# Summing the squares of the last RMS norm on TensorE, block by block, instead of on VectorE

## The chip, the cores and the metric

The kernel runs on one core of a Trainium2 chip. The metric is the device time of one execution in microseconds. Times of several runs are given by their median. A core has TensorE (matmuls, shown as PE, with its weight loads as PEld), VectorE (DVE), ScalarE (ACT), GpSimd (POOL) and SyncE (SP), each with its own queue in program order; they wait for each other by semaphores.

## The reference, cut to what matters

The program is two transformer blocks on 512 tokens of 1024 features. The second ends with a mixture of 16384 experts (PEER), whose output is added to the residual `x`, and the kernel ends with an RMS norm:

```
def rmsnorm_2(x, g):
    xf = x.astype(jnp.float32)
    y = xf * lax.rsqrt(jnp.mean(xf * xf, axis=-1, keepdims=True) + EPS)
    return (y * g.astype(jnp.float32)).astype(x.dtype)
...
        x = x + peer_ffn(h2, peer_w_query[l], peer_sub_keys[l], peer_u[l], peer_v[l])
    return rmsnorm_2(x, final_g)
```

All that changes is how the sum over the 1024 features of `xf * xf` is formed, once per token.

## The kernel before, in words

The residual is kept transposed in SBUF: `xT` has 128 partitions (features) x KD = 8 blocks x T = 512 tokens. So the squares of a token lie on 128 partitions in 8 blocks, and their sum goes over both.

The last stage adds the experts' output. It goes over 64 pairs of expert tiles (N_PAIRS). For each pair j, `mix` on TensorE makes the 8 blocks of the output with 6 matmuls each (L1786 to L1788, 128 x 128 stationary, 416 moving columns), into banks 0 to 3 in turn, and counts `y_done`. VectorE adds each block to `xT` and counts `y_added` (L1698, and L1772 for the last pair). ScalarE meanwhile prepares the next weights.

Behind the last pair comes the final norm. ScalarE squares block k as soon as its residual addition is done (`square_tile`, L765) into one of three buffers: block 0 into `sq[:, 0]`, the others in turn into `sq[:, 1]` and `res`; from the third buffer's reuse on it waits for VectorE (`sq_added`). VectorE adds block k - 1 of squares to `sq[:, 0]` behind the residual addition of block k (`add_square`, L1238), seven additions in all. When the seventh is done (`squares`), TensorE sums over the partitions: `square_sums` (L1883) has one matmul for each 128 tokens, with the squares as the stationary operand and one column of ones as the moving one, and leaves four columns of bank 4. ScalarE takes the root (L699, with a table load), VectorE the reciprocal (L1174), TensorE spreads it over all partitions (`spread_roots`, L1875, four matmuls with 128 moving columns into bank 5), VectorE makes the eight final products (L1779), and ScalarE's queue stores each block when it is done (L1114).

Every engine runs its queue in order. On TensorE the final norm's instructions stand behind the matmuls of pair 63. The four buffers `rows[0..3]` (128 x 1024 each) take gathered expert rows in an earlier part of the stage; ScalarE waits for `acc_added` before it comes to the final norm.

Of the kernel before, what the change touches and what calls it, by code (L numbers as in the profile page):

```python
# [26 lines left out]
ACT = mybir.ActivationFunctionType  # L27
AX_X = mybir.AxisListType.X

P = 128  # L30
D = 1024
KD = D // P
T = 512
TT = T // P
# [162 lines left out]
def program(nc, x, stream, gains, consts, rel, gqa, keys, ohc, rows_u, rows_v, out):  # L197
    ctx = ExitStack()
    with ctx:
# [3 lines left out]
        def fixed(name, shape, dt=F32):  # L203
            size = int(np.prod(shape[1:])) * (2 if dt in (BF16, F16) else 4)
            if size % ROW == 0:
                at[0] = -(-at[0] // ROW) * ROW
            t = nc.alloc_sbuf_tensor_at(name, shape, dt, offset=at[0])
            at[0] += -(-size // 32) * 32
            return t

        def sem(name):
            return ctx.enter_context(nc.semaphore(name))


        xT = fixed("xT", [P, KD, T])
# [9 lines left out]
        rr = fixed("rr", [P, TT])  # L225
# [123 lines left out]
        rows = [fixed(f"rows{r}", [P, D]) for r in range(ROWS_AHEAD - 1)]  # L349
# [36 lines left out]
                    2: sq[:, 0, :], 3: sq[:, 1, :], 4: rt[:, 0, :], 5: pr1[:, 1, 0, :]}  # L386
        y_scaled = pr1[:, 0, 0, :]
        normed_of = lambda k: (res[:, :], rt[:, 0, :], sq[:, 1, :])[k % 3]
        sq_tile = lambda k: sq[:, 0, :] if k == 0 else sq[:, 1, :] if k % 2 else res[:, :]
        spilled = nc.dram_tensor("spilled", (N_SPILLED, P, DT), F32, kind="Internal").ap()  # L390
        gates = nc.dram_tensor("gates", (N_SPILL, P, NKEY, SPILL), F32, kind="Internal").ap()

        banks = ctx.enter_context(nc.psum_tensor("bank", [P, 8, T], F32))
        B = [banks[:, i, :] for i in range(8)]
# [13 lines left out]
        roots = sem("roots")  # L408
        recips = sem("recips")
# [77 lines left out]
        acc_turned = sem("acc_turned")  # L487
        acc_added = sem("acc_added")
        a_moved = sem("a_moved")
        gate_done = sem("gate_done")  # L490
        high_w = sem("high_w")

        ident = cs[:, CC["ident"]:CC["ident"] + P]
        ones = cs[:, CC["ones"]:CC["ones"] + P]
# [17 lines left out]
        def gain(name, k=0):  # L512
            return gn[:, GC[name] + k:GC[name] + k + 1]
# [162 lines left out]
        def _(act):  # L676
# [19 lines left out]
            def root_of(width, scale, n_sums):  # L696

                act.wait_ge(sums, n_sums)
                act.activation(rr[:, :width], B[4][:, :width], ACT.Sqrt, bias=gain("eps"), scale=scale).then_inc(roots, 1)  # L699
# [61 lines left out]
            def square_tile(nth, k, src=xT):  # L761

                if k >= 3:
                    act.wait_ge(sq_added, nth * (KD - 2) + k - 2)
                act.activation(sq_tile(k), src[:, k, :], ACT.Square).then_inc(squared, 1)  # L765
# [10 lines left out]
            n_sums = KD  # L776
# [87 lines left out]
            for m in range(AHEAD, N_IN2):  # L864
# [11 lines left out]
                o = 2 * g + r - 2 if m < 4 * KD else m - 2 * KD  # L876
# [230 lines left out]
            for k in range(KD):  # L1107

                act.wait_ge(y_added, (N_PAIRS - 1) * KD + k + 1)
                square_tile(2, k)  # L1110
            root_of(TT, 1.0 / D, n_sums + KD)
            for k in range(KD):
                act.wait_ge(final_done, k + 1)
                act.dma_start(out[:, k, :], xT[:, k, :]).then_inc(out_done, 16)  # L1114
# [4 lines left out]
        def _(dve):  # L1119
# [52 lines left out]
            def over_root(width, nth_root):  # L1172
                dve.wait_ge(roots, nth_root)
                dve.reciprocal(rr[:, :width], rr[:, :width]).then_inc(recips, 1)  # L1174
# [58 lines left out]
            def add_square(nth, k):  # L1233

                dve.wait_ge(squared, nth * KD + k + 1)
                if k >= 2:
                    dve.wait_ge(sq_added, nth * (KD - 2) + k - 1)
                ins = dve.tensor_tensor(sq_tile(0), sq_tile(0), sq_tile(k), ALU.add)  # L1238
                if k < KD - 1:
                    ins.then_inc(sq_added, 1)  # L1240
                else:
                    ins.then_inc(squares, KD)

            n_sums, n_root, n_spread = 0, 0, 0
# [267 lines left out]
            for k in range(KD):  # L1512
                t = c2[:, k, :]
# [256 lines left out]
            for k in range(KD):  # L1770
                dve.wait_ge(y_done, (N_PAIRS - 1) * KD + k + 1)
                dve.tensor_tensor(xT[:, k, :DT], xT[:, k, :DT], B[k % 4][:, :DT], ALU.add).then_inc(y_added, 1)  # L1772
                if k >= 2:
                    add_square(2, k - 1)
            add_square(2, KD - 1)
            over_root(TT, n_root + 1)
            dve.wait_ge(spread, n_spread + 1)
            for k in range(KD):
# [4 lines left out]
        def _(pe):  # L1783
# [87 lines left out]
            def spread_roots(bank=5):  # L1871

                for t in range(TT):
                    tok = slice(t * P, (t + 1) * P)
                    m = pe.matmul(B[bank][:, tok], rr[:, t:t + 1].broadcast_to([P, P]), ident, start=True, stop=True)  # L1875
                m.then_inc(spread, 1)

            def square_sums(n):


                pe.wait_ge(squares, n + KD)
                for t in range(TT):
                    m = pe.matmul(B[4][:, t:t + 1], sq[:, 0, t * P:(t + 1) * P], ones[:, 0:1], start=True, stop=True)  # L1883
                m.then_inc(sums, KD)

            def full_norm(n, nth):

                square_sums(n)
                pe.wait_ge(recips, nth)
                spread_roots()  # L1890
# [82 lines left out]
            n_sq, n_rt = 0, 0  # L1973
# [298 lines left out]
            for n in range(NB):  # L2272
                build(n)
                while at_step < tile_steps(n):
                    u, k = at_step // KD, at_step % KD
# [17 lines left out]
            def mix(j, wpar, n_lo, r):  # L2293

                pe.wait_ge(lo_done, n_lo)
                pe.wait_ge(w_done, j * 2 + 2)
                for k in range(KD):
                    if not isinstance(j, int) or j * KD + k - 3 > 0:
                        pe.wait_ge(y_added, j * KD + (k - 3))
                    c = slice(k * P, (k + 1) * P)  # L2300
                    for e in (0, 1):
                        m = mm3(B[k % 4][:, :DT], hi[:, r + e, c], lo[:, r + e, c], WH[:, wpar, e, :DT], WL[:, wpar, e, :DT],
                                e == 0, e == 1)
                    m.then_inc(y_done, 1)
# [54 lines left out]
            with pe.Fori(N_BOTH // 2, N_PAIRS // 2) as i:  # L2359
                for q in (0, 1):  # L2360
                    mix(i * 2 + q, q, i * 4 + (S_LAST - 2 * N_BOTH + 2 * q + 2), 2 * q)
            full_norm(n_sq, n_rt + 1)

        return None

# [120 lines left out]
```

## Time and profile before

| what | value |
|---|---|
| median of 3 runs | 2484.57 us (2475.71 to 2488.78) |
| profiled execution, its own time | 2480.68 us |
| its span | 2478.8 us |
| TensorE matmul busy | 2406.5 us (97%) |
| VectorE busy | 1686.6 us (68%) |
| ScalarE busy | 929.7 us (38%) |
| last wide matmul to the end of the span | 13.7 us |

The span runs from the first to the last record of the core; the own time includes what lies around it. Busy time is the union of an engine's instructions, and the durations of overlapping matmuls are more than their spacing. The trace shows two records (a load and a matmul, twice) for each 4-byte matmul of the final norm, so 4 matmuls appear as x8.

### The profile page before, as it was taken

What the parts mean: (1) busy time and instruction counts of PE and PEld (TensorE: products, weight loads), DVE (VectorE), ACT (ScalarE), POOL (GpSimd) and SP (SyncE); (2) the same over time, 40 slices, a digit from 0 to 9 for tenths busy, and PEclk for the clock granted to TensorE, in tenths of its full rate; (3) what the DMA queues carried; (4) which work ended last, traced back from release to release, by engine and by line L of the source; (5) the groups of instructions that cost most, each with busy time, mean ns of one, the idle gap of its engine ahead of it and who ended that gap; (6) DMA issues with size and microseconds to landing.
All of it is one profiled execution on the core that took longest, in us unless ns stands there. A gap on an engine that the chain in (4) does not pass through costs nothing.

```text
span 2478.8 us, 37450 instructions
## 1 busy us (share of the span) xinstructions
PE 2406.5 (97%) x13120; PEld 2162.0 (87%) x13120; DVE 1686.6 (68%) x3411; ACT 929.7 (38%) x1473; POOL 1333.1 (54%) x1185
## 2 busy tenths in 40 slices
PE   7999999999999999999998998999999999999998
PEld 6785788888888886788997887999999999999998
DVE  6476733332499977779999975666766766666666
ACT  3146222222322346414354553333333433433443
POOL 5520565656555562464410014777777777777553
PEclk9999999999999999999999998999999999999999
DMA  4210233223233222122225676877887887887552
GB/s 170 94 52 27 77 102 100 94 102 102 86 109 100 95 85 80 50 97 85 96 92 188 250 267 190 297 250 277 271 272 270 274 282 264 269 282 263 172 168 96
DMA packets 210870, 402.72 MB, mean 162 GB/s; under 512 B 118336, under 2 KB 123840, under 8 KB 207424
## 3 DMA queue, kind: packets, MB, share of 16 engines
q1 hardware_dynamic: 64224, 233.36, 28.1%
q0 software_dynamic: 27648, 100.68, 11.0%
q10 hardware_dynamic: 118880, 67.18, 9.1%
q8 instruction: 66, 1.08, 0.2%
q14 instruction: 52, 0.43, 0.1%
HBM read 369.25 MB, written 31.92 MB: 162 GB/s over the span
## 4 chain that ended last, share of the span: by engine, by line
PE 74%; DVE 17%; issue 3%; POOL 3%; ACT 1%; DMA 1%; DVEq 0%; POOLq 0%; SPq 0%; ACTq 0%
PE bank L1786 23%; PE bank L1787 23%; PE bank L1788 23%; POOL lo L600 3%; DVE ohg L1667 2%; DVE lo L1606 1%; DVE oh L1663 1%; DVE oh L1664 1%; PE bank L1944 1%; PE bank L1955 1%; PE bank L1931 1%; DVE idx L1565 1%; DVE inH L1133 1%; DVE idx L1557 1%; DVE scb L1558 1%
## 5 line engine op out<-in xcount | busy, mean ns | idle before, releaser
L600 POOL TENSOR_TENSOR lo<-raw,hi 128x256 fp32r<-128x256 f32 (+1 forms) x950 | 1135.2, 1224 | 1006.8 <-ACT hi L686 562.5
L1786 PE MATMUL bank<-inH,hi 128*128 128x512 f32 (+1 forms) x2112 | 790.2, 374 | 19.2 <-DVE inL L1134 14.0
L1788 PE MATMUL bank<-inH,lo 128*128 128x512 f32 (+1 forms) x2112 | 781.5, 370 | 0.0
L1787 PE MATMUL bank<-inL,hi 128*128 128x512 f32 (+1 forms) x2112 | 781.2, 370 | 0.0
L1786 PEld LDWEIGHTS bank<-inH,hi 128*128 128x128 f32 x2112 | 396.5, 188 | 69.5 <-issue 17.7
L1698 DVE TENSOR_TENSOR xT<-xT,bank 128x416 f32<-128x416 f32 x504 | 288.7, 582 | 220.0 <-PE bank L1788 218.5
L1788 PEld LDWEIGHTS bank<-inH,lo 128*128 128x128 f32 x2112 | 396.5, 188 | 43.0
L1787 PEld LDWEIGHTS bank<-inL,hi 128*128 128x128 f32 x2112 | 396.9, 188 | 41.9 <-issue 0.2
L686 ACT ACTIVATE hi<-raw 128x1024 fp32r<-128x1024 f32 x232 | 243.7, 1056 | 407.4 <-PE bank L1788 396.2
L1786 PE MATMUL bank<-WH,hi 128*128 128x416 f32 x1024 | 358.3, 350 | 12.0 <-DVE WL L1694 12.0
L1787 PE MATMUL bank<-WL,hi 128*128 128x416 f32 x1024 | 357.6, 349 | 0.0
L1788 PE MATMUL bank<-WH,lo 128*128 128x416 f32 x1024 | 357.5, 349 | 0.0
L1020 ACT ACTIVATE hi<-raw 128x1024 fp32r<-128x1024 f32 x180 | 184.1, 1048 | 216.0 <-PE bank L1788 216.0
L1786 PEld LDWEIGHTS bank<-WH,hi 128*128 128x128 f32 x1024 | 192.6, 188 | 12.6 <-issue 12.3
L1787 PEld LDWEIGHTS bank<-WL,hi 128*128 128x128 f32 x1024 | 192.6, 188 | 0.3
L1788 PEld LDWEIGHTS bank<-WH,lo 128*128 128x128 f32 x1024 | 192.5, 188 | 0.3
L1689 DVE TENSOR_TENSOR bank<-bank,Gd 128x416 f32<-128x416 f32 x128 | 76.0, 594 | 120.0 <-ACT bank L1030 120.0
L1484 DVE SCALAR_TENSOR_TENSOR bank<-u,gn,bank 128x512 f32<-128x512 f32 x224 | 148.2, 748 | 0.0
L1720 DVE SCALAR_TENSOR_TENSOR bank<-rows,gate_sp,bank 128x1024 f32<-128x1024 f32 x93 | 119.2, 1281 | 1.3
L1046 ACT ACTIVATE A<-bank 128x416 f32<-128x416 f32 x84 | 43.5, 518 | 204.0 <-PE bank L1788 204.0
L1707 DVE CUSTOM_DVE_ANT_0 rows<-bank,rows 128x1024 f32<-128x1024 f32 x96 | 116.0, 1218 | 0.0
L1035 ACT ACTIVATE WH<-bank 128x416 fp32r<-128x416 f32 x128 | 65.5, 512 | 109.1 <-DVE bank L1689 109.1
(324 smaller groups left out, 2919.0 us busy)
## 6 DMA issues: line engine op xcount, KB each, us to landing
raw<-stream SPq DMA_DIRECT2D x440, 512.0 KB, 3.3
Gd<-gates ACTq DMA_DIRECT2D x32, 832.0 KB, 6.3
gates<-stage_a ACTq DMA_DIRECT2D x13, 1024.0 KB, 4.3
gates<-stage_b ACTq DMA_DIRECT2D x13, 1024.0 KB, 5.0
tbl<-gqa ACTq DMA_DIRECT2D x8, 384.0 KB, 3.2
spilled<-res ACTq DMA_DIRECT2D x12, 208.0 KB, 4.2
A<-spilled ACTq DMA_DIRECT2D x6, 416.0 KB, 3.3
xT<-x SPq DMA_DIRECT2D x4, 512.0 KB, 8.8
```

The lines of the kernel that those rows point to most:

```text
L600: ins = pool.tensor_tensor(lo[:, r, part], raw[:, r, part], hi[:, r, part].bitcast(F32), ALU.subtract)
L686: act.activation(hi[:, r % RING, :], raw[:, r % RING, :], ACT.Copy).then_inc(hi_done, 1)
L1020: act.activation(hi[:, r, :], raw[:, r, :], ACT.Copy).then_inc(hi_done, 1)
L1035: act.activation(WH[:, j % 2, e, :DT], staged(j, e), ACT.Copy).then_inc(high_w, 1)
L1484: done.append(chain.mark(dve.scalar_tensor_tensor(to, *tap(j), d, ALU.mult, ALU.add)))
L1689: dve.tensor_tensor(a, a, Gd[:, buf, :, 2 * (j % 2) + e, :], ALU.mult).then_inc(gate_done, 1)
L1698: dve.tensor_tensor(xT[:, k, :DT], xT[:, k, :DT], B[k % 4][:, :DT], ALU.add).then_inc(y_added, 1)
L1707: dve.tensor_tensor_reduce(out=rows[r][:, :], in0=held, in1=rows[r][:, :], scale=1.0, scalar=0.0, op0=ALU.mult, op1=ALU.add, accum_out=dot ...
L1720: dve.scalar_tensor_tensor(held, rows[r][:, :], weight, held, ALU.mult, ALU.add).then_inc(row_used, 1)
L1786: pe.matmul(bank, wh, xh, start=start, stop=False)
L1787: pe.matmul(bank, wh, xl, start=False, stop=False)
L1788: return pe.matmul(bank, wl, xh, start=False, stop=stop_)
```

## The change

The eight blocks of squares get a buffer each: halves of `rows[0..3]`. ScalarE no longer waits for VectorE between squares. VectorE adds no squares. TensorE sums each block over the partitions as it comes, with four one-column matmuls for each block that accumulate over the eight blocks in column 0 of banks 4 to 7, one bank for each 128 tokens. ScalarE's root reads these four columns.

```
         normed_of = lambda k: (res[:, :], rt[:, 0, :], sq[:, 1, :])[k % 3]
+        last_square = lambda k: rows[k // 2][:, k % 2 * T:(k % 2 + 1) * T]
...
+        last_squared = sem("last_squared")
+        last_sums = sem("last_sums")
...
                 act.wait_ge(y_added, (N_PAIRS - 1) * KD + k + 1)
-                square_tile(2, k)
-            root_of(TT, 1.0 / D, n_sums + KD)
+                act.activation(last_square(k), xT[:, k, :], ACT.Square).then_inc(last_squared, 1)
+            act.wait_ge(last_sums, TT)
+            act.activation(rr[:, :TT], banks[:, 4:4 + TT, 0:1].rearrange("p b o -> p (b o)"), ACT.Sqrt, bias=gain("eps"), scale=1.0 / D).then_inc(roots, 1)
...
                 dve.tensor_tensor(xT[:, k, :DT], xT[:, k, :DT], B[k % 4][:, :DT], ALU.add).then_inc(y_added, 1)
-                if k >= 2:
-                    add_square(2, k - 1)
-            add_square(2, KD - 1)
             over_root(TT, n_root + 1)
...
-            full_norm(n_sq, n_rt + 1)
+            for k in range(KD):
+                pe.wait_ge(last_squared, k + 1)
+                for t in range(TT):
+                    m = pe.matmul(B[4 + t][:, 0:1], last_square(k)[:, t * P:(t + 1) * P], ones[:, 0:1], start=k == 0, stop=k == KD - 1)
+                    if k == KD - 1:
+                        m.then_inc(last_sums, 1)
+            pe.wait_ge(recips, n_rt + 1)
+            spread_roots()
```

## Rows read from the trace of the kernel before

**Rows 1.** The page's slices, 40 equal parts: TensorE's granted clock in tenths.

```profile
PEclk9999999999999999999999998999999999999999
```

**Rows 2.** Chain of waits from 2464 us: start us, us, what.

```profile
2464.58 0.68 DVE sq L1238
...
2466.53 0.70 DVE sq L1238
...
2467.28 1.08 PE bank L1883 x8
...
2468.91 2.09 PE bank L1875 x8
```

**Rows 3.** Timeline of the tail: start us, us, engine, line, operation [idle before <- releaser].

```profile
2464.62 0.35 PE L1787 MATMUL bank<-WL,hi 128*128 128x416 f32 x1
...
2464.70 0.63 ACT L765 ACTIVATE res<-xT 128x512 f32<-128x512 f32 x1 [0.49 <-DVE xT L1772]
2464.81 0.34 PE L1788 MATMUL bank<-WH,lo 128*128 128x416 f32 x1
2465.19 0.59 DVE L1772 TENSOR_TENSOR xT<-xT,bank 128x416 f32<-128x416 f32 x1
...
2465.82 0.63 ACT L765 ACTIVATE sq<-xT 128x512 f32<-128x512 f32 x1 [0.48 <-DVE xT L1772]
2466.46 1.28 ACT L699 ACT_TABLE_LOAD   x1
...
2467.28 1.07 PE L1883 MATMUL bank<-cs,sq 128*128 128x1 f32 x8 [2.12 <-DVE sq L1238]
2468.39 0.26 ACT L699 ACTIVATE rr<-bank,gn 128x4 f32<-128x4 f32 x1 [0.64 <-PE bank L1883]
...
2468.91 2.08 PE L1875 MATMUL bank<-cs,rr 128*128 128x128 f32 x8 [0.56 <-DVE rr L1174]
...
2469.29 1.70 PE L1875 MATMUL bank<-cs,rr 128*128 128x128 f32 x7
...
2471.03 5.36 DVE L1779 SCALAR_TENSOR_TENSOR xT<-xT,gn,bank 128x512 f32<-128x512 f32 x8 [2.17 <-PE bank L1875]
```

**Rows 4.** Groups by line, 2467.2 to 2471.1 us: busy us, mean ns of one.

```profile
L1875 PE MATMUL bank<-cs,rr 128*128 128x128 f32 x8 | 2.1, 441 | 0.6 <-DVE rr L1174 0.6
...
L1883 PE MATMUL bank<-cs,sq 128*128 128x1 f32 x8 | 1.1, 255 | 2.1 <-DVE sq L1238 2.1
```

**Rows 5.** Timeline of TensorE near 32 us: the first norm's sums behind wide matmuls.

```profile
32.04 0.39 PE L1788 MATMUL bank<-inH,lo 128*128 128x512 f32 x1
32.27 0.95 PE L1883 MATMUL bank<-cs,sq 128*128 128x1 f32 x8
```

**Rows 6.** Timeline of TensorE near 1548 us: 16 small passes between wide matmuls.

```profile
1547.56 1.05 PE L2314 MATMUL bank<-cs,res 128*128 128x128 f32 x8
...
1549.26 0.44 PE L1786 MATMUL bank<-WH,hi 128*128 128x416 f32 x1
```

**Rows 7.** Timeline of TensorE near 952 us, 64 stationary columns at half clock.

```profile
952.06 1.12 PE L1955 MATMUL bank<-pT,v 128*64 128x128 f32 x8
```

**Rows 8.** Stretches: from:to, length, PE busy (count), granted clock, DMA share, GB/s.

```profile
2465.10:2468.10 3.00, 0.88 (x9) 1.00 0.00 0
2468.20:2471.10 2.90, 2.23 (x10) 0.50 0.00 0
186.60:188.00 1.40, 0.00 (x0) 1.00 0.00 0
188.20:194.00 5.80, 5.80 (x24) 0.50 0.01 1
1487.60:1491.90 4.30, 0.00 (x0) 1.00 0.73 240
1492.00:1499.40 7.40, 0.00 (x0) 0.50 0.96 261
943.00:949.10 6.10, 3.26 (x28) 1.00 0.24 86
949.30:955.00 5.70, 5.43 (x29) 0.50 0.25 69
```

## The prediction

> **What bounds the kernel now.** I began with the page's slices [rows 1]: TensorE's granted clock is full nearly everywhere and the engine is busy, so the body of the kernel is a matmul stream that this change does not touch. Everything edited lies behind the last pair of experts. So I read the chain of waits for the last 15 us [rows 2] and the timeline of the same stretch [rows 3]. The reader is to see a serial tail: the last wide matmul (2464.81 to 2465.15), VectorE's last residual addition (2465.19), ScalarE's last square (2465.82 to 2466.45), VectorE's last addition of squares (2466.53), four sums on TensorE (2467.28 to 2468.35), the root, the reciprocal, the spread (2468.91 to 2470.99), eight final products with their stores. Whatever moves the end of the four sums moves the end of the kernel one for one, because nothing runs beside that stretch. For the price of a small matmul I took the grouped lines of the tail [rows 4], an early place where the same sums stand behind wide matmuls [rows 5], a run of 16 small passes in mid-kernel [rows 6] and a run with half as many stationary columns at the low clock [rows 7]. For the clock I took the stretches before and after four of its falls [rows 8].
>
> **The change, part by part.**
>
> *VectorE's seven additions of squares go.* Each is about 0.69 us [rows 2]. Six of them hide beside the last pair's matmuls: the residual addition of block 7 starts at 2465.19, 0.04 us after its matmul ends [rows 3], so it is paced by TensorE already. The seventh is on the path: between the end of the last square (2466.45) and the first sum (2467.28) lie 0.83 us, and these go. ScalarE's waits on those additions go too. They cost nothing now: the last square starts 0.04 us after its residual addition ends. So square 7 still ends at 2466.45, and square 6 at 2465.33 [rows 3].
>
> *TensorE gets eight times the sums.* Before: 4 matmuls, which the trace shows as 8 passes (each of these matmuls is two loads and two matmuls). After: 8 x 4 = 32 matmuls, 64 passes. They stand in TensorE's queue behind all matmuls of the last pair, and so none of them can run beside that pair. The wide passes follow each other by 0.19 us, so the first sum can run at 2464.81 + 0.19 = 2465.00. By then squares 0 to 5 are there. Square 6 (2465.33) and square 7 (2466.45) are wanted after 48 and 56 passes, 5 us later. None of the eight waits stalls, and nothing is queued behind them but other sums.
>
> *The price of a pass at the full clock.* A row's duration (0.255 us [rows 4]) is not its spacing, because passes overlap. In the tail, 8 passes take 1.07 us, so the spacing is (1.07 - 0.255) / 7 = 0.116. Behind wide matmuls it is (0.95 - 0.25) / 7 = 0.10 [rows 5]. The sixteen 128-column passes of line 2314 run from 1547.56 to 1549.26, 0.106 each [rows 6]. One moving column or 128 cost the same, so the load of 128 stationary columns sets the spacing. I take 0.11. A pass that stands alone adds 0.25 at the end.
>
> *The price at half clock.* The spread's last seven passes take 1.70 us: (1.70 - 0.42) / 6 = 0.213 [rows 3], where 0.42 is about the duration of one (the mean is 0.441 with the longer first [rows 4]). No row has one moving column at half clock. From below it cannot be under the full clock's 0.11; from above 0.213. I take 0.213, because the load sets the spacing: with 64 stationary columns in place of 128, and the same 128 moving ones, it is (1.12 - 0.42) / 7 = 0.10 at half clock [rows 7], half of 0.213.
>
> The Trainium skill ("TensorE: Matmul & The Clock Gate", LDWEIGHTS) gives a load as its columns over 1.2, 107 ns for 128, whatever the clock. At the full clock the trace agrees (0.11). By that rule a fall of the clock would cost nothing here and the sums would give +3.8; the rows of the spread, which have 128 moving columns too, speak for twice the spacing at half clock.
>
> *Where the clock is.* Now it holds full until 2468.1 and is at half (1.2 of 2.4 GHz) from 2468.2 on, about 3.1 us after the last wide matmul, with 0.88 us of TensorE work between [rows 8]. After other dense stretches it fell sooner and later: between 1.4 and 1.6 us after the work ended (188), 4.4 us after (1492), and some 6.2 us after the wide matmuls had given way to a stretch with 3.26 us of work in 6.1 (949). A stream of one-column passes without a gap is nowhere in the trace. I assume that it does not hold the clock, since the array has almost nothing to multiply, and place the fall where it is now, at 2468.2.
>
> *The sum.* From 2465.00 to 2468.2 at 0.11: 29 passes. The 30th starts at 2468.19, and 34 more spacings of 0.213 put the 64th at 2475.43; with 0.42 it ends at 2475.85. Now the sums end at 2468.35. The difference is +7.5 us. It contains the gain: the sums start 2.28 us earlier, and last 10.85 instead of 1.07 us.
>
> *Root and rest.* The root now reads one element from each of four banks, still four elements a partition: 0.26 us as now. Its table load (2466.46 to 2467.74 [rows 3]) is issued straight after the last square, while the sums run; it stays hidden behind them. If the sums got short it would cost up to 1.3 us. Reciprocal, spread, products, stores: unchanged, the spread at the same half clock. Two more semaphores and eight squares in four row buffers, which the last gathered row has long left, cost nothing.
>
> The profiled execution has a span of 2478.8 and its own time is 2480.68. That becomes 2480.68 + 7.5 = 2488.2. The median of the runs is 3.89 above that execution, 2484.57, so I predict 2484.57 + 7.5 = **2492.1**.
>
> **Rivals.**
>
> *A: the stream holds the clock.* For it: TensorE is never without an instruction, and the clock survived gappy work for 6 us before 949 [rows 8]. Against: there the clock fell in the end, with TensorE at work for half of the time on far wider passes than these. Price: the 64th pass starts at 2465.00 + 63 x 0.11 = 2471.93 and ends at 2472.18, +3.8; the spread's 8 passes then take about 1.07 instead of 2.08, -1.0. Together +2.8: 2487.4. The skill's page on TensorE ("Why this matters for your kernels") asks only that there be no long idle gaps between bursts, by which the clock would hold here; the rows of the tail, in which the fall came with a gap of 2.1 us and a light burst, bear neither reading out. Chance 0.28.
>
> *B: my forecast,* the clock falls inside the sums. Fall after 1.5 us: 14 passes before it, end 2477.4, +9.05. After 6.3 us: 57 before it, +4.6. All at half clock: 2465.00 + 63 x 0.213 + 0.42 = 2478.84, +10.5. Chance 0.61.
>
> *C: passes much cheaper than now,* because loads overlap as those of line 1955 do. At the lowest spacing I could take from a row, 0.10 with 64 stationary columns, nothing is won; the sums break even at (2468.35 - 2465.00 - 0.25) / 63 = 0.049 a pass, and with the spread at full clock at 0.065. That is about half of every 128-column row. At 0.049, 2484.6, no change; if the passes cost less still, at most the 3.35 us would be won. Chance 0.04.
>
> *D: slower by more than can be missed.* Passes that don't overlap. The change sends consecutive matmuls to banks 4, 5, 6, 7 in turn and adds to them again each fourth, where now all four go to one bank. If that serialised them, a pass would cost its whole duration, 0.255: 2465.00 + 64 x 0.255 = 2481.3, +13.0, 2497.5, and at half clock up to 28.2 us of sums, +24.9. It decides over 0.5% from 0.246 a pass. Against it: the wide matmuls change their bank every six passes and accumulate without a gap. Chance 0.07.
>
> **How the numbers follow.** What a measurement of this kernel can tell from no change is 0.5%, 12.4 us; its three runs lie 13 us apart. Cases A, B and C all lie within it. The likeliest, B, has +4.6 to +10.5, which is 2489.2 to 2495.1; with A it reaches down to 2487.4. The scatter of a median of such runs, some 4 us from the runs shown, comes on either side: 2483 to 2498. Slower by over 0.5%: most of D and a little of B with scatter, 0.06. Faster: scatter alone, 0.02. Same: 0.92.
>
> **What would show it.** In the new profile the sums' line should have 64 passes, its first at the heels of the last wide matmul, without a wait on ScalarE or VectorE, spaced 0.11 and from some point 0.21; the granted clock should fall to half inside them; no addition of squares after the last residual; the table load hidden behind the sums; sums ending about 10.9 us after 2465.00's counterpart against 3.35 now; the tail behind them as now. I am wrong on the clock if it stays full through the spread (then +2.8), wrong on the spacing if it is 0.11 at half clock too (then about +3.8), and wrong on the order if TensorE waits for a square in mid-stream.

## The result, and the profile after

The changed kernel takes 2491.56 us (median of 14 runs, 2486.16 to 2496.22) against 2484.11 us before (14 runs, 2475.71 to 2488.78): 7.45 us more, ratio 1.0034, 95% interval 1.0023 to 1.0044. That is slower by a little, inside the 0.5% that the prediction called no change, and 0.5 us from the predicted 2492.1. The interval stands for +5.7 to +10.9 us, so that the forecast and the measurement lie closer together than the runs can tell is luck.

The profiled execution has a span of 2490.9 us. The chain of waits of its last 21 us, which answers to [rows 2], has no VectorE addition of squares any more, and one piece of TensorE work where three engines took turns (start us, us, what):

```profile
2470.00 10.40 PE bank L2366 x55
...
2480.42 0.27 ACT rr L1115
...
2480.72 0.19 DVE rr L1178
...
2480.95 2.09 PE bank L1876 x8
```

The timeline of the same stretch answers to [rows 3] (L2366 are the new sums, L1115 the root, L1876 the spread):

```profile
2468.75 0.35 PE L1789 MATMUL bank<-WH,lo 128*128 128x416 f32 x1
2468.94 11.45 PE L2366 MATMUL bank<-cs,rows 128*128 128x1 f32 x64
2469.14 0.59 DVE L1776 TENSOR_TENSOR xT<-xT,bank 128x416 f32<-128x416 f32 x1 [0.55 <-PE bank L1789]
2469.76 0.63 ACT L1113 ACTIVATE rows<-xT 128x512 f32<-128x512 f32 x1 [0.51 <-DVE xT L1776]
2470.41 1.28 ACT L1115 ACT_TABLE_LOAD   x1
2480.42 0.26 ACT L1115 ACTIVATE rr<-bank,gn 128x4 f32<-128x4 f32 x1 [8.73 <-PE bank L2366]
...
2480.95 2.08 PE L1876 MATMUL bank<-cs,rr 128*128 128x128 f32 x8 [0.56 <-DVE rr L1178]
...
2468.94 2.70 PE L2366 MATMUL bank<-cs,rows 128*128 128x1 f32 x23
...
2471.49 8.89 PE L2366 MATMUL bank<-cs,rows 128*128 128x1 f32 x41
```

The sums start 0.19 us behind the start of the last wide matmul and run without a gap for 11.45 us. ScalarE is done with the last square at 2470.39 and with the table load at 2471.69; then it waits 8.73 us. The last two lines cut the 64 passes in two. The first 23 are spaced (2.70 - 0.25) / 22 = 0.111 us, the other 41 (8.89 - 0.35) / 40 = 0.213, where 0.25 and 0.35 are the durations of the last pass in each. What lies between is seen in the stretches (from:to, length, PE busy, granted clock, DMA share, GB/s), which answer to [rows 8]:

```profile
2469.00:2471.30 2.30, 2.30 (x23) 1.00 0.00 0
2471.50:2480.30 8.80, 8.80 (x42) 0.50 0.00 0
```

In what follows the measure is the **tail**: from the start of the last wide matmul to the start of the root. It was 3.58 us (2464.81 to 2468.39 [rows 3]) and is 11.67: +8.09. Nearly all the rest of the 12.1 us between the two spans is in the body: the last wide matmul starts 3.94 us later. The experiments take both up.

### The profile page after: what moved, and what is told of

Same layout as the page of the kernel before. It is cut to its first block, busy times and chain, and to the rows that moved or that the text cites. A ratio compares the mean times of both kernels' runs of the same rounds, so it can differ in the third digit from the quotient of the medians.

```text
span 2490.9 us, 37544 instructions
## 1 busy us (share of the span) xinstructions
PE 2422.3 (97%) x13176; PEld 2173.8 (87%) x13176; DVE 1679.0 (67%) x3404; ACT 929.7 (37%) x1473; POOL 1333.8 (54%) x1185
## 3 DMA queue, kind: packets, MB, share of 16 engines
q0 software_dynamic: 27648, 100.68, 10.9%
## 4 chain that ended last, share of the span: by engine, by line
PE 74%; DVE 17%; issue 3%; POOL 3%; ACT 1%; DMA 1%; DVEq 0%; POOLq 0%; ACTq 0%; SPq 0%
PE bank L1787 23%; PE bank L1788 23%; PE bank L1789 23%; POOL lo L603 3%; DVE ohg L1671 2%; DVE lo L1610 1%; DVE oh L1667 1%; DVE oh L1668 1%; PE bank L1945 1%; PE bank L1956 1%; PE bank L1932 1%; DVE idx L1569 1%; DVE inL L1138 1%; DVE idx L1561 1%; DVE scb L1562 1%
## 5 line engine op out<-in xcount | busy, mean ns | idle before, releaser
L1787 PEld LDWEIGHTS bank<-WH,hi 128*128 128x128 f32 x1024 | 193.1, 189 | 13.7 <-issue 12.5
```

What stands on the lines that cost most here:

```text
L1787: pe.matmul(bank, wh, xh, start=start, stop=False)
```

## The experiments

The theory: a sum costs its passes, 0.11 us each at the full clock and 0.213 at half; the clock falls a few us after the last wide matmul, whatever the one-column passes do; nothing else of the change has a price. Each rival puts the price elsewhere: in the buffers or the missing waits, in the number of moving columns, in the banks, in stalls, or in the body.

**The buffers alone.** VectorE adds as before, from eight buffers:

```
+                act.activation(last_square(k), xT[:, k, :], ACT.Square).then_inc(squared, 1)
...
+                ins = dve.tensor_tensor(sq_tile(0), last_square(0) if k == 1 else sq_tile(0), last_square(k), ALU.add)
```

> One part of the change alone: ScalarE writes the eight squares into eight buffers and waits for nobody, but VectorE still adds them and TensorE sums once, as before. Theory (the whole loss is in TensorE's 56 added passes): from the start of the last wide matmul to the start of the root 3.6 us as before, the last square 0.04 us after its residual addition. Rival (eight buffers, or squares without a wait, cost something by themselves): over 4 us.

The tail is 3.56 us. Timeline:

```profile
2470.33 0.34 PE L1797 MATMUL bank<-WH,lo 128*128 128x416 f32 x1
...
2472.80 1.05 PE L1892 MATMUL bank<-cs,sq 128*128 128x1 f32 x8 [2.12 <-DVE sq L1776]
2473.89 0.26 ACT L700 ACTIVATE rr<-bank,gn 128x4 f32<-128x4 f32 x1 [0.62 <-PE bank L1892]
...
2474.41 1.16 PE L1884 MATMUL bank<-cs,rr 128*128 128x128 f32 x8 [0.57 <-DVE rr L1175]
```

So in this profile buffers and ScalarE's freedom are worth nothing either way. Two more readings: the spread takes 1.16 us here and 2.08 before [rows 3], at the same code, because in this execution the clock was still full; and the last wide matmul starts at 2470.33, 5.5 us later than before, at the same body.

**128 moving columns.** One edit in the changed kernel:

```
-                    m = pe.matmul(B[4 + t][:, 0:1], last_square(k)[:, t * P:(t + 1) * P], ones[:, 0:1], start=k == 0, stop=k == KD - 1)
+                    m = pe.matmul(B[4 + t][:, 0:P], last_square(k)[:, t * P:(t + 1) * P], ones[:, 0:P], start=k == 0, stop=k == KD - 1)
```

> The changed kernel with 128 moving columns of ones in place of one in each sum (the same sum lands in 128 columns, the root reads one). Theory (the load of 128 stationary columns sets the spacing): 0.11 us a pass at full clock and 0.213 at half, as with one column; if the clock falls as before, root starts 11 to 12.5 us after the last wide matmul starts. Rival (moving columns matter at half clock, the one-column pass is cheaper there): spacing above 0.213 at half clock. Rival on the clock (a gapless stream of wider passes holds it): full clock to the end of the sums, root after 7.5 us, spread 1.1 instead of 2.1 us.

The tail is 7.54 us, 4.1 less than with one column. Timeline, then stretches:

```profile
2467.85 0.35 PE L1789 MATMUL bank<-WH,lo 128*128 128x416 f32 x1
2468.04 7.31 PE L2366 MATMUL bank<-cs,rows 128*128 128x128 f32 x64
...
2475.39 0.26 ACT L1115 ACTIVATE rr<-bank,gn 128x4 f32<-128x4 f32 x1 [4.59 <-PE bank L2366]
...
2475.92 1.16 PE L1876 MATMUL bank<-cs,rr 128*128 128x128 f32 x8 [0.56 <-DVE rr L1178]
```

```profile
2468.10:2475.30 7.20, 7.20 (x65) 1.00 0.00 0
...
2477.20:2480.60 3.40, 0.00 (x0) 1.00 0.56 216
2480.90:2484.90 4.00, 0.00 (x0) 0.50 0.81 313
```

The spacing is (7.31 - 0.275) / 63 = 0.112, that of one column at the full clock. More columns cost nothing per pass at the full clock, and during this stream and the spread the clock stayed full: the rival on the clock came true, for 128 columns, and the theory's figure of 11 to 12.5 us missed. The rival on the spacing at half clock was not put to the test here; the spread's passes with 128 columns (0.213 [rows 3]) and the sums' with one (0.213) answer it.

**One bank, nothing accumulated.** 32 separate sums into 32 columns of bank 4. The root reads the last block's four, so this kernel leaves the sum over the other seven blocks out.

```
+                    m = pe.matmul(B[4][:, k * TT + t:k * TT + t + 1], last_square(k)[:, t * P:(t + 1) * P], ones[:, 0:1], start=True, stop=True)
```

> The changed kernel with its 32 sums into 32 columns of one bank, none adding to another; the root reads the four sums of the last block, so the sum over the other seven blocks is left out. Theory (load and clock set the spacing): 0.11 and 0.213, root after 11 to 12.5 us as in the changed kernel. Rival (alternating over four banks, or accumulating, costs): spacing at half clock clearly under 0.213 or at full clock under 0.10, root 1 us or more earlier.

The tail is 9.18 us, under the range that I gave, and by more than the 1 us that I had given the rival. Stretches, and the timeline of the passes after the fall:

```profile
2466.40:2471.40 5.00, 5.00 (x47) 1.00 0.00 0
2471.70:2475.30 3.60, 3.60 (x18) 0.50 0.00 0
```

```profile
2471.59 3.77 PE L2366 MATMUL bank<-cs,rows 128*128 128x1 f32 x17
```

(3.77 - 0.35) / 16 = 0.214 a pass at half clock, and 5.0 us of full clock hold some 46 passes, 0.11 each. Spacing as with four banks; what was earlier is due to the clock, which here fell only 5.3 us after the start of the last wide matmul. So the rival's figure came true without its mechanism, and the banks are out.

**Every sum twice.** 128 passes, the second 64 overwriting the first.

```
+            for again in (0, 1):
+                for k in range(KD):
```

> The changed kernel with its 32 sums made twice over (the second time overwrites the first), 128 passes. Theory: the added 64 passes all run at half clock at 0.213, +13.6 us against the changed kernel, root 25.3 us after the last wide matmul starts, ratio to the kernel before 1.0087. Rival (a long stream of small passes brings the clock back): part of them at 0.11, at the least +7 us.

Ratio to the kernel before 1.0090, interval 1.0070 to 1.0111; tail 24.94 us, 0.4 under the theory's. Timeline, then stretches:

```profile
2462.99 24.72 PE L2367 MATMUL bank<-cs,rows 128*128 128x1 f32 x128
```

```profile
2463.00:2465.80 2.80, 2.80 (x27) 1.00 0.00 0
2466.10:2487.70 21.60, 21.60 (x102) 0.50 0.00 1
```

27 passes at full clock, 101 after. 27 x 0.11 + 101 x 0.213 = 24.5 us, and the line shows 24.72. So the rival fell: a gapless stream of one-column passes did not bring the clock back in 21.6 us.

**The sums inside the last pair.** The last two pairs are taken out of the loop, and block k's sums stand behind the matmuls of block k + 1 (`after` is the function of block k's sums):

```
                     m.then_inc(y_done, 1)
+                    if after and k:
+                        after(k - 1)
```

> The changed kernel with the sums of block k placed in TensorE's queue behind the matmuls of block k + 1 of the last pair, so that only block 7's stand behind them all. Theory: no pass runs at half clock; 48 passes at 0.11 lengthen the last pair by 5.3 us, then block 6's eight passes hide the wait for the last square, and the root starts 2.8 us after the last wide matmul starts; with the spread at full clock about +3.5 us against the kernel before, some 4.5 us better than the changed kernel. Rival (TensorE waits for squares in the middle of the pair): over 0.3 us idle in front of a block's sums and a loss near that of the changed kernel.

Ratio 1.0030, interval 1.0017 to 1.0042. The clock stayed full until the last sums were done, as expected, and was at half in the spread; the tail is 2.96 us. Stretches, then the timeline of three blocks' sums:

```profile
2476.00:2478.60 2.60, 2.04 (x18) 1.00 0.00 0
2478.90:2481.50 2.60, 2.08 (x8) 0.50 0.00 0
```

```profile
2463.80 1.05 PE L2366 MATMUL bank<-cs,rows 128*128 128x1 f32 x8 [0.29 <-ACT rows L1113]
...
2467.95 0.95 PE L2366 MATMUL bank<-cs,rows 128*128 128x1 f32 x8
...
2469.97 0.95 PE L2366 MATMUL bank<-cs,rows 128*128 128x1 f32 x8
```

A block now takes 2.02 us (2467.95 to 2469.97) against 1.12, 0.90 more, and at the first one TensorE waits for its square, so the six cost 5.9 us. Minus 0.62 in the tail, and the spread at half clock in both profiles: +5.3. I had +3.5: the wait (0.45) and the spread at full clock (0.9) were most of what I missed. The theory also had this kernel some 4.5 us better than the changed one. By the tail and the pair it is 2.3 to 2.8 better (+5.3 against +7.6 and +8.1), and by the ratios (1.0030 against 1.0034 and 1.0027) no gain can be told. Without any sum at half clock the change still loses, because a pass costs 0.11 us at the full clock inside the pair too (0.90 / 8).

**Fewer passes, three ways.** Pairs of blocks added by VectorE (32 passes); VectorE's sum of blocks 0 to 5, and 6 and 7 alone (24 passes); the changed kernel with squares in the rounded type, which the trace shows as one load and one matmul an instruction (32 passes in all). One piece of each edit, in this order:

```
+                dve.tensor_tensor(last_square(k), last_square(k), last_square(k - 1), ALU.add).then_inc(two_added, 1)
...
+            for k in (0, *range(N_ADDED, KD)):
+                pe.wait_ge(*((last_squared, k + 1) if k else (on_added, N_ADDED - 1)))
...
+                act.activation(lastR[:, k, :], xT[:, k, :], ACT.Square).then_inc(last_squared, 1)
```

> The changed kernel, but VectorE adds the squares of blocks 1, 3, 5, 7 to those of their neighbours, and TensorE sums four tiles (32 passes), all behind the last pair. Theory: the last tile is ready 0.83 us after the last square; 24 passes fill the time to it and beyond, 2.6 us, then 8 more: root 3.9 to 4.8 us after the last wide matmul starts, +0.3 to +1.2 against the kernel before, by when the clock falls. Rival (the passes are cheap beside the wait for the clock or the squares): under 3.6 us.

> VectorE adds the squares of blocks 0 to 5 as before; TensorE sums that tile and the squares of blocks 6 and 7 by themselves, 24 passes. Theory: the first eight start when VectorE's tile is ready, 0.5 us after the last wide matmul starts, no gap until the end: 0.5 + 24 x 0.11 + 0.15 = 3.3 us to the root, against 3.6 before. Rival (a part of them at half clock or a wait between): 3.6 us or more.

> The changed kernel with the squares written in the rounded 4-byte type that the trace shows as one load and one matmul for each instruction, against a column of ones of the same type (two columns wide). Theory (passes are what costs): 32 passes, root 3.8 us after the last wide matmul starts if the clock holds that long and 4.5 if it falls after 2.4 us. Rival (each instruction has a fixed price whatever its passes): 7 us or more.

Tails 3.85, 3.38 and 3.85 us. The sums' lines in the three timelines:

```profile
2468.09 3.63 PE L2375 MATMUL bank<-cs,rows 128*128 128x1 f32 x32
```

```profile
2472.11 2.84 PE L2377 MATMUL bank<-cs,rows 128*128 128x1 f32 x24
```

```profile
2470.93 3.63 PE L2370 MATMUL bank<-WL,lastR 128*128 128x2 f32 x32
```

32 passes take 3.63 us, 0.11 each, whether they are 16 instructions of two or 32 of one: what counts is the pass. In all three profiles the clock was still full when the sums were done. Five additions kept on VectorE beat the kernel before by 0.2 us in the tail, in one profile of each.

**What the runs pointed to.** The last two ways together, and one root of a constant ahead of the squares, so that the table load leaves the tail:

```
+            act.activation(act_sp[:, :TT], xT[:, 0, DT:DT + TT], ACT.Sqrt, bias=gain("eps"), scale=0.0)
...
+            for k in range(N_ADDED - 1, KD):
...
+                    m = pe.matmul(B[4 + t][:, 0:2], lastR[:, k, t * P:(t + 1) * P], WL[:, 0, 0, DT:DT + 2], start=k == N_ADDED - 1, stop=k == KD - 1)
```

> Built from what the runs showed, against the kernel before: VectorE adds the squares of blocks 0 to 5 (the last addition rounds its result), TensorE sums that tile and the rounded squares of blocks 6 and 7 in 12 passes, and ScalarE takes one root of a constant ahead of the squares, so that the table is there. Theory: the last four passes start when the last square is done, and the root starts 2.4 us after the last wide matmul starts, against 3.58: -1.2 us, and by where the clock falls 0.9 us more or less at the spread. Ratio 0.9995, too small for the runs to tell. Rival (the table is loaded again behind the squares): root at 2.9 us.

```profile
2457.25 1.28 ACT L1115 ACT_TABLE_LOAD   x1
...
2469.26 0.35 PE L1806 MATMUL bank<-WH,lo 128*128 128x416 f32 x1
...
2469.76 1.80 PE L2383 MATMUL bank<-WL,lastR 128*128 128x2 f32 x12
2470.27 0.63 ACT L1119 ACTIVATE lastR<-xT 128x512 fp32r<-128x512 f32 x1 [0.50 <-DVE xT L1791]
2471.60 0.26 ACT L1121 ACTIVATE rr<-bank,gn 128x4 f32<-128x4 f32 x1 [0.70 <-PE bank L2383]
```

The tail is 2.34 us, 1.24 under the kernel before. The table load has moved ahead of all squares (2457.25), and none stands between square and root. The ratio is 0.9997, interval 0.9984 to 1.0010: the gain is seen in the trace and is below what the runs can tell.

**The 128 columns timed, and the changed kernel beside it.**

> The changed kernel with 128 moving columns, as in the look before, now timed. Theory (at 128 columns the stream holds the clock in every run, and so the wider sums are the faster ones): full clock to the end of the sums, root 7.5 us after the last wide matmul starts, ratio to the kernel before 1.0012 to 1.0016, under that of the changed kernel. Rival (the clock held by chance in that one look): it falls inside the sums, ratio 1.003 as the changed kernel.

> The changed kernel itself beside the two others on one chip. Theory: clock falls between 2 and 6 us after the last wide matmul, root after 8.8 to 12 us, ratio 1.002 to 1.0035. Rival (part of the loss is in the body of the kernel, where the first profile of it was 3.9 us longer too): the last wide matmul later than in the kernels with the same body on this chip by some 4 us again.

128 columns: ratio 1.0015 (1.0004 to 1.0027), tail 7.53, full clock to the end of the spread again. The changed kernel itself: 1.0027 (1.0014 to 1.0039; one of its 12 runs took 9903 us and is left out), tail 11.19. The two intervals overlap, and the two medians are both 2487.9 us: that the wider sums are faster is read from the tails, in two profiles of each, and the runs do not tell the two kernels apart. Their stretches:

```profile
2469.60:2476.80 7.20, 7.20 (x65) 1.00 0.00 0
```

```profile
2471.20:2474.00 2.80, 2.80 (x27) 1.00 0.00 0
2474.30:2482.00 7.70, 7.70 (x37) 0.50 0.00 0
```

As for the body: over the eleven profiles of changed forms that have the same work ahead of the last wide matmul (all but the one with sums inside the pair), it starts between 2462.80 (every sum twice) and 2471.61 (six blocks added). The changed kernel's own two are at 2468.75 and 2471.00, the one profile of before at 2464.81. Forms with the same matmuls in the body thus lie up to 8.8 us apart, and the kernel before was profiled in an execution 3.4 us under its median of 14 (2480.68), the changed one in an execution 1.1 us over its own (2492.68). That is 4.5 us between the profiled executions, which covers the body's 3.94. In the second profile of the changed kernel the last wide matmul starts 1.7 us later than in the two other forms profiled beside it (2469.26 and 2469.34), not the rival's 4, and that execution was 6.5 us over its median. The two ratios say 8.4 and 6.7 us, the two tails 8.1 and 7.6. With intervals of some 3 us either way, a small part in the body can't be excluded; none is needed.

## Why the prediction was right, point by point

- **What is bounded by what.** Right: the tail is serial, and the end of the sums moved the end of the kernel.
- **Waits.** Right: none of the eight waits stalls, the first sum stands 0.19 us behind the last wide matmul, and the table load is hidden. The buffers alone changed nothing.
- **The price of a pass.** Right at both clocks: 0.111 and 0.213 us, where I had 0.11 and, between 0.11 and 0.213, had taken the upper end. The moving columns don't set it: one and 128 have the same spacing at either clock. That the load of the 128 stationary columns does is argued from this and from [rows 7] (half the spacing with 64 of them); no run of these sums had fewer. The Trainium skill ("TensorE: Matmul & The Clock Gate", LDWEIGHTS) has the columns over 1.2 for such a load, 107 ns for 128, and names no clock beside it: as a spacing the trace agrees at the full clock and not at half, where 101 passes in a row are spaced 0.213. A smaller slip: the last pass at half clock lasts 0.35 and not the 0.42 that the sum took from the spread.
- **The clock.** Right in kind, and the one term that was mis-sized by much. I let it fall 3.2 us after the first sum; in the profile it fell 2.4 us after it (2468.94 to about 2471.4), so 23 passes and not 29 ran at the full clock, and the sums took 11.45 us instead of 10.85. Over four profiles of streams of 64 or more one-column passes (the changed kernel twice, one bank, every sum twice) the fall came 2.6, 3.1, 5.3 and 3.0 us after the last wide matmul's start, always inside the stream. In the seven profiles with fewer than 64 passes behind that matmul, with and without gaps, it came 2.8 to 5.4 us after it: no effect of the one-column stream on the moment of the fall is seen. That the array's idleness is the reason, as the prediction assumed, no run shows; they show one moving column against 128, and no count between them for 64 passes.
- **The kernel before as a yardstick.** One step was too simple: I took its spread as always at half clock. With the buffers alone and with VectorE adding pairs it ran at the full clock, 1.16 us. So some executions of the kernel before may well take 0.9 us less than its profile shows, which no trace of it settles; in neither of the changed kernel's two profiles was the clock still full there.
- **Rivals.** A (the stream holds the clock) did not happen at one column; its price, +2.8 with the faster spread, is what 128 columns gave: +3.96 in the tail and 0.92 less in the spread, +3.0. The Trainium skill ("TensorE: Matmul & The Clock Gate", "Why this matters for your kernels") advises against idle gaps between bursts, by which A would have held: this trace does not agree, since the stream had no gap and the granted clock fell to 0.50 in it. C and D fell with the measured spacing and with the single bank.

## What to carry to other kernels

Moving a reduction to TensorE in this form costs its passes, one for each load of 128 stationary columns, whatever the moving columns at a given clock. Six additions that hide beside matmuls are free; 56 passes behind the last matmul are not. The other form, with the ones stationary and the squares moving, was not run. At the end of a dense stretch, price TensorE's work at half clock unless the trace shows otherwise, and reduce the number of passes first.

## What the runs showed of the hardware that I had not expected

- The sums with more work per pass were done sooner: 64 passes with 128 moving columns took 7.31 us, with one column 11.45, 10.97 and 8.96, because the granted clock stayed at 2.4 GHz in the one (two profiles of two) and fell to 1.2 GHz in the other (three of three, and in the stream of 128 passes). With 128 columns it fell 12.8 and 13.1 us after the start of the last wide matmul, 3.6 and 3.9 us after the end of the spread.
- TensorE never idle is not enough to bring the clock back: 21.6 us of back-to-back one-column passes stayed at half.
- The moment of the fall moved by 2.7 us between executions of like streams (2.6 to 5.3 us after the start of the last wide matmul), which is worth 2.5 us of the tail (11.67 against 9.18).
- ScalarE's squares after a root of a constant needed no new table load, nor did the root after them (the load at 2457.25, 1.28 us, is the last one of that profile).
